# Attention inside a fused diffusion-backbone layer: the score maxima of two heads taken by products on rows 0 to 63 and 64 to 127 of the array, in six pairs of banks per half query tile

## What is computed

```python
def one(qblk):                       # 128 queries at a time
    s = jnp.einsum('bqkgd,bskd->bkgqs', qblk, k).astype(jnp.float32) * scale
    p = jax.nn.softmax(s, axis=-1).astype(v.dtype)
    return jnp.einsum('bkgqs,bskd->bqkgd', p, v)
```

## Time and profile before

| | |
|---|---|
| median of 3 runs | 2532.43 us (2530.58 to 2535.45) |
| the profiled execution | 2528.88 us, its span 2527.0 us |
| TensorE busy | 2432.8 us (96% of the span) |
| VectorE, ScalarE, GpSimd busy | 1187.3, 678.1, 155.7 us |
| mean granted TensorE clock | 0.985 of full speed |
| the attention's groups | 1190.76 to 1441.80 us from the span's start |

### The profile page before, as it was taken

How to read it: one execution, slowest core, us unless ns; L and a number is a source line. 1 busy time by engine, 2 the same in 40 slices (tenths; PEclk the granted TensorE clock), 3 DMA queues, 4 the chain that set the end, 5 groups by cost and what they waited for, 6 DMA issues and landing times. The chain is left out here.

```text
span 2527.0 us, 41706 instructions
## 1 busy us (share of the span) xinstructions
PE 2432.8 (96%) x17387; PEld 2240.3 (89%) x17387; DVE 1187.3 (47%) x1773; ACT 678.1 (27%) x1036; POOL 155.7 (6%) x194
## 2 busy tenths in 40 slices
PE   6999999999999999989999999979999999999998
PEld 4887789999999899888999898869999999999997
DVE  3331111003543667645555476445555555555555
ACT  3321111113332232234444453232112112112112
POOL 0000000001100011112111010110000000000000
PEclk8999999999999999999999999989999999999999
DMA  6224532225453333142002093231011011011012
GB/s 264 107 84 175 196 121 82 97 70 186 165 176 115 134 116 113 56 131 74 17 17 83 19 388 107 99 142 42 33 50 41 33 50 41 33 50 41 33 50 84
DMA packets 98125, 247.19 MB, mean 98 GB/s; under 512 B 12593, under 2 KB 56065, under 8 KB 88657
## 3 DMA queue, kind: packets, MB, share of 16 engines
q1 hardware_dynamic: 61200, 174.69, 20.0%
q10 hardware_dynamic: 32832, 55.46, 5.9%
q0 software_dynamic: 3968, 15.21, 1.6%
HBM read 183.85 MB, written 61.55 MB: 97 GB/s over the span
## 5 line engine op out<-in xcount | busy, mean ns | idle before, releaser
L59 PE MATMUL ps<-zb,wt 128*128 128x384 f32 x2400 | 651.5, 337 | 10.4 <-DVEq L2617 9.1
L59 PEld LDWEIGHTS ps<-zb,wt 128*128 128x128 f32 x2400 | 441.6, 188 | 28.4 <-DVEq L2617 9.5
L2569 DVE TENSOR_TENSOR merged<-merged,ps 128x512 f32<-128x512 f32 x378 | 259.5, 687 | 322.7 <-PE ps L59 320.1
L59 PE MATMUL ps<-xb,wt 128*128 128x384 f32 x1056 | 358.5, 340 | 0.0
L59 PE MATMUL ps<-ys 128*128 128x512 f32 x1056 | 298.2, 394 | 0.0
L59 PE MATMUL ps<-h_hi,fill_whi 128*128 128x384 f32 x672 | 234.7, 349 | 7.0 <-PEq L79 3.6
L59 PE MATMUL ps<-h_hi,fill_wlo 128*128 128x384 f32 x672 | 225.8, 336 | 0.0
L59 PE MATMUL ps<-h_lo,fill_whi 128*128 128x384 f32 x672 | 225.6, 336 | 0.0
L59 PEld LDWEIGHTS ps<-xb,wt 128*128 128x128 f32 x1056 | 198.5, 188 | 17.3
L59 PEld LDWEIGHTS ps<-ys 128*128 128x128 f32 x1056 | 193.3, 188 | 16.6
L59 PE MATMUL ps<-prj_whi,h_hi 128*128 128x512 f32 (+1 forms) x432 | 164.9, 382 | 6.1 <-DVE h_lo L553 6.1
(11 more groups left out here) (348 smaller groups left out, 3708.3 us busy)
## 6 DMA issues: line engine op xcount, KB each, us to landing
wraw<-in_w_ffn_in SPq DMA_DIRECT2D x22, 1024.0 KB, 4.8
prj_raw<-in_w_ada SPq DMA_DIRECT2D x16, 1024.0 KB, 5.9
fill_raw<-in_w_fill SPq DMA_DIRECT2D x30, 512.0 KB, 4.2
bg_dram<-fill_st ACTq DMA_DIRECT2D x72, 192.0 KB, 2.0
xf<-bg_dram POOLq DMA_DIRECT2D x24, 576.0 KB, 7.9
tok_dram<-prj_tst ACTq DMA_DIRECT2D x45, 256.0 KB, 2.1
zf<-in_w_ffn_out SPq DMA_DIRECT2D x22, 512.0 KB, 3.5
prj_raw<-in_w_tok SPq DMA_DIRECT2D x10, 1024.0 KB, 6.5
```

The source lines that it names most:

```text
L59: mm = pe.matmul(out, lhs[a], rhs[b], start=first and n == 0, stop=last and n == 2)
L2569: v.tensor_tensor(dst, dst, ps[:, bank, :], ALU.add).then_inc(added, 1)
```

## The change

`shift_scores` now works on two heads at once. `qpart` is laid out anew, so that after turning the even head of a pair has the high part of its queries on rows 0 to 63, and the odd head on rows 64 to 127. The keys' high part stands on both halves already. A call ("event" below) makes two products of 64 rows and 384 columns, one for each head, into banks 0 and 1, for one third of the keys. There are six events per group instead of four, at steps 1, 2, 3, 5, 6 and 7. The products no longer take in the low part of the queries, so the maxima differ slightly; any value near the maximum serves, since it only shifts the exponent. VectorE reduces the two banks after each event to one maximum per head and third; after events 2 and 5 it reduces the thirds to one, and negates. `split` takes five instructions instead of two.

```diff
-        qpart = [ph.sb(f"qpart{i}", [P, G, H2], F32R) for i in range(KV)]
+        QP = 5 * HD + 2
+        qpart = [ph.sb(f"qpart{i}", [P, G // 2, QP], F32R) for i in range(KV)]
...
-            def shift_scores(n, kv, a):
-
-                if not (isinstance(n, int) and n + a == 0):
-                    pe.wait_ge(sem["mx"], 4 * n + a)
-                for c in SHIFTS:
-                    mm = pe.matmul(ps[:, c, 0:TH], qt[kv][:, a * P:a * P + P], kt[0][:, kv, c * TH:c * TH + TH],
+            def shift_scores(n, kv, e):
+
+                if not (isinstance(n, int) and n + e == 0):
+                    pe.wait_ge(sem["mx"], 6 * n + e)
+                p, c = divmod(e, 3)
+                for b in range(2):
+                    r, at = slice(b * HD, b * HD + HD), slice((2 * p + b) * P, (2 * p + b) * P + P)
+                    mm = pe.matmul(ps[:, SHIFT + b, 0:TH], qt[kv][r, at], kt[0][r, kv, c * TH:c * TH + TH],
                                    start=True, stop=True)
                 mm.then_inc(sem["s1"], 1)
...
-            for a in range(G):
-                shift_scores(0, 0, a)
-                branch(range(20 + a, 21 + a))
+            for e in range(6):
+                shift_scores(0, 0, e)
+                if e % 3 < 2:
+                    u = 20 + e // 3 * 2 + e % 3
+                    branch(range(u, u + 1))
             shifts(0, 0, 1)
...
-                x = qr[:].rearrange("p (a k) d -> p k a d", k=KV)[:, kv]
-                link(v.tensor_copy(qpart[kv][:, :, 1:H1], x))
-                v.tensor_tensor(qpart[kv][:, :, H1:H2], x, qpart[kv][:, :, 1:H1].bitcast(F32), ALU.subtract).then_inc(done, 1)
+                x = qr[:].rearrange("p (a b k) d -> p k a b d", k=KV, b=2)[:, kv]
+                at = lambda i: qpart[kv][:, :, i:i + HD]
+                even, odd = x[:, :, 0], x[:, :, 1]
+                link(v.tensor_copy(at(0), even))
+                link(v.tensor_copy(at(4 * HD + 1), odd))
+                link(v.tensor_copy(at(2 * HD), even))
+                link(v.tensor_tensor(at(HD), even, at(0).bitcast(F32), ALU.subtract))
+                v.tensor_tensor(at(3 * HD + 1), odd, at(4 * HD + 1).bitcast(F32), ALU.subtract).then_inc(done, 1)
...
-            def shift(n, kv, a):
-
-                v.wait_ge(sem["s1"], 4 * n + a + 1)
-                v.tensor_reduce(mx[:, a % 2:a % 2 + 1], ps[:, 0:3, 0:TH], AX.XY, ALU.max).then_inc(sem["mx"], 1)
-                v.wait_ge(sem["mx"], 4 * n + a + 1)
-                v.tensor_scalar(qpart[kv][:, a, 0:1], mx[:, a % 2:a % 2 + 1], -1.0, None, ALU.mult).then_inc(sem["nm"], 1)
+            def shift(n, kv, e):
+
+                p, c = divmod(e, 3)
+                v.wait_ge(sem["s1"], 6 * n + e + 1)
+                v.tensor_reduce(mx3[:, p, :, c], ps[:, SHIFT:SHIFT + 2, 0:TH], AX.X, ALU.max).then_inc(sem["mx"], 1)
+                if c == 2:
+                    v.wait_ge(sem["mx"], 6 * n + e + 1)
+                    link(v.tensor_reduce(mx[:, p], mx3[:, p], AX.X, ALU.max))
+                    v.tensor_scalar(qpart[kv][:, p, 3 * HD:5 * HD + 2:2 * HD + 1], mx[:, p], -1.0, None, ALU.mult).then_inc(sem["nm"], 1)
...
-                        for a in range(G):
-                            shift(2 * i + kv + 1, 1 - kv, a)
-                            if kv and more2 and a == 1:
+                        for e in range(6):
+                            shift(2 * i + kv + 1, 1 - kv, e)
+                            if kv and more2 and e == 2:
                                 norm_a(i + 3)
-                            if kv and more2 and a == 2:
+                            if kv and more2 and e == 3:
                                 norm_b(i + 3, qtab[:, bass.ds(i + 2, 1)].rearrange("p a c d -> p (a c) d"))
```

More of the change, by code:

```diff
@@ L1558, in attention @@
         pt = [ph.sb(f"pt{i}", [P, G * P]) for i in range(3)]
-        mx = ph.sb("mx", [P, 2])
+        mx3, mx = ph.sb("mx3", [P, 2, 2, 3]), ph.sb("mx", [P, 2, 2])
         rs = ph.sb("rs", [P, KV, G])
@@ L1568, in attention @@
         PT, ST, OB = 3, 4, 7
-        SHIFTS = range(0, 3)
+        SHIFT = 0
+        EVENTS = (1, 2, 3, 5, 6, 7)
         use = lambda i, k: 2 + 5 * i + k
@@ L1648, in turn_queries @@
             for a in range(G):
-                mm = pe.transpose(ps[:, bank, a * P:a * P + P], qpart[kv][:, a, 1:H2].bitcast(F32), g.ident[:])
+                at = a % 2 * (3 * HD + 1)
+                mm = pe.transpose(ps[:, bank, a * P:a * P + P], qpart[kv][:, a // 2, at:at + 2 * HD].bitcast(F32), g.ident[:])
             return mm
@@ L1653, in turn_shifts @@
             for a in range(G):
-                mm = pe.transpose(ps[0:H1, bank, a * P:a * P + P], qpart[kv][:, a, 0:H1].bitcast(F32), g.ident[:])
+                at = 2 * HD if a % 2 == 0 else 4 * HD + 1
+                mm = pe.transpose(ps[0:H1, bank, a * P:a * P + P], qpart[kv][:, a // 2, at:at + H1].bitcast(F32), g.ident[:])
             return mm
@@ L1739, in shifts @@
             def shifts(n, kv, u):
-                pe.wait_ge(sem["nm"], 4 * n + 4)
+                pe.wait_ge(sem["nm"], 2 * n + 2)
                 pe.wait_ge(sem["pte"], u)
@@ L1782, in group @@
                     scores(n, kv, j)
-                    if more and j in (1, 3, 5, 7):
-                        a = j // 2
-                        if a == 0:
+                    if more and j in EVENTS:
+                        e = EVENTS.index(j)
+                        if e == 0:
                             pe.wait_ge(sem["pte"], u + 1)
-                        shift_scores(n + 1, nkv, a)
+                        shift_scores(n + 1, nkv, e)
                     if j >= 2:
@@ L2003, in _ @@
             for kv in range(KV):
-                link(v.tensor_copy(qpart[kv][:, :, 0:1], zero[:]))
+                for i in (3 * HD, 5 * HD + 1):
+                    link(v.tensor_copy(qpart[kv][:, :, i:i + 1], zero[:, 0:2]))
             link(v.tensor_tensor(qr[:], qn[:], grow[:, 0, :].unsqueeze(1).broadcast_to([P, AH, HD]), ALU.mult))
@@ L2065, in tile @@
                     if kv == 0 or more:
-                        for a in range(G):
-                            shift(2 * i + kv + 1, 1 - kv, a)
-                            if kv and more2 and a == 1:
+                        for e in range(6):
+                            shift(2 * i + kv + 1, 1 - kv, e)
+                            if kv and more2 and e == 2:
                                 norm_a(i + 3)
-                            if kv and more2 and a == 2:
+                            if kv and more2 and e == 3:
                                 norm_b(i + 3, qtab[:, bass.ds(i + 2, 1)].rearrange("p a c d -> p (a c) d"))
                     normed(2 * i + kv, kv)
-            for a in range(G):
-                shift(0, 0, a)
+            for e in range(6):
+                shift(0, 0, e)
             with v.Fori(0, 6) as i:
-                link.loop(i, 4)
+                link.loop(i, 14)
                 tile(i, True, True)
```

4 lines of the change are left out of this document (2 added, 2 removed).

## The result

| | before | after |
|---|---|---|
| median of the runs | 2533.61 us (2530.58 to 2536.11, 6 runs) | 2770.14 us (2756.98 to 2771.86, 6 runs) |
| the profiled execution | 2528.88 us, span 2527.0 us | 2757.54 us, span 2755.7 us |
| mean granted TensorE clock | 0.985 | 0.905 |

The ratio is 1.0918 (95% interval 1.0903 to 1.0933): the kernel is 9% slower. I had said 2567 us, range 2544 to 2584. The sign was right, the size was not: 237 us more instead of 35.

What follows compares the result with a forecast made beforehand. TensorE, busy throughout each group at full clock, was taken as the bound. 15 groups add 30.2 us and the part ahead of the loop 4.4: 34.6 on 2528.88, 2563.5; the median lies 3.55 higher: 2567 us, range 2544 to 2584.

Steps and rivals of the forecast that it cites:

- An event's 0.58 us, side by side: TensorE, each event: two half-row products overlap, 0.17 us for the pair, 0.58 with shape changes and unhidden weights (0.47 to 0.69).
- serial: Rival: the pair's products run one after the other, 0.17 us more per event, 2579 us; chance 0.13.
- The change of shape: TensorE around each event: 0.10 us into the narrow shape, 0.10 back, 0.10 for the next full weights, unhidden.
- That rival (2545): Rival: the change of shape costs nothing and the pair takes 0.17 us, but waits grow: 2545 us; chance 0.18.
- VectorE's part: VectorE in each group: `split` 1.42 us instead of 0.75, reductions 0.96 us; TensorE waits only at event 1.
- Event 1 waits as forecast: TensorE at each group's second event waits 0.83 us for VectorE's reduction, net 0.72; no waits at later events.
- A group at full clock: Each loop group gets 2.0 us longer (1.29 events, 0.72 wait), 17.6 to 18 us apart; 15 groups, 30.2 us.
- Ahead of the loop: Before the group loop: events 1.1 us, event 3's wait 1.2, `shifts` 1.4, longer `split` 0.67; together 4.4 us.
- The 0.67 us of the longer `split`: Ahead of the loop: the first queries already wait 0.87 us for `split`, so its 0.67 more come on top.
- The step that failed: All loop groups: pieces were priced at the earlier trace's full clock, giving 30.2 us over 15 groups.
- a clock that falls because TensorE idles, which none of my cases has: Sign named for a wrong prediction, in the profile after: TensorE's clock falls through idling; given no size or chance.

Runs made afterwards that it cites:

- a kernel that only adds them: Kernel before with one 128-column product per head for the maxima, plus six unread half-row pairs per group: 2557.06 us, ratio 1.0098.
- one-row product added: Kernel before plus six products of one row and 128 columns of zeros in each group, ahead of the scores: 2560.56 us, ratio 1.0114.
- the full-row twin: Kernel before with one 128-column product per head for maxima, plus six unread all-row pairs per group: 2537.43 us; with 7 us pause ahead of loop 2553.3 us.
- the pause: TensorE waits about 7 us for four GpSimd powers ahead of the loop; added to the kernel before: 2540.8 us, ratio 1.0034.
- the short version: Kernel before with one product of 128 columns per head for the maxima, cached keys only: 2506.13 us, ratio 0.99.
- the version with the short products and a pause of 7 us: Kernel before with one 128-column product per head for maxima, six unread half-row pairs per group and the pause: 2787.64 us, ratio 1.0998.
- the four short products that did not save it: Changed kernel plus one unread product of all 128 rows and 128 columns in steps 1, 3, 5, 7 of each group: 2767.14 us, ratio 1.0904.
- the one-row products: Six per group, kernel before with fewer maxima columns: one of three products, 2546.07 us; one 128-column product, seven runs 2532.49 to 2538.88, three 2678.36 to 2732.6.
- ten runs of one version: Kernel before with one 128-column product per head for the maxima, plus six one-row products per group: seven runs 2532.49 to 2538.88 us, three 2678.36 to 2732.6.

## Why the prediction was right in its pieces and wrong in its size

- **An event's 0.58 us, side by side**: right, 0.58 in the group at full clock, 0.53 on average in a kernel that only adds them. The side by side was open (chance 0.13 for serial): same rows 0.62 us, both halves 0.45. **The change of shape** (0.30): right, 0.29 us taken away with `nil`, 0.24 per one-row product added, its columns left out. That rival (2545) falls.
- **VectorE's part**: right in its times, too high in its cost. `split` 1.40 us (forecast 1.42), the reduction 0.95 (0.96). Event 1 waits as forecast, but adds 0.47 and 0.56 us in the two groups at full clock, not 0.72. In the loop the weight loads of events wait for VectorE 15 times, 10.2 us in all; only in these two groups does the wait hold up the products.
- **A group at full clock**: 17.62 us from one `nil` to the next, where before has 16.01 and 15.62 by turns. That is 1.8 more than their mean, where the sum had 2.0: 1.29 for the events, and the shorter wait. The forecast was 17.6 to 18.
- **Ahead of the loop**: event 3 waits 1.06 us (1.2), `shifts` 1.46 (1.4). The 0.67 us of the longer `split` did not come on top: the first queries wait 0.88, and ScalarE's copy ends it. From the first event to these queries it is 18.37 us against 14.73: 3.6 more, where I had 4.4. Both stretches contain the dip of the clock of 6.8 us.
- **The step that failed** is the one on which the sum rests, that every group runs at the clock of the earlier trace rows. Among what would make the prediction wrong I had put "a clock that falls because TensorE idles, which none of my cases has". It needed a case, with a price: 15 groups at 30.7 us instead of 17.6, and what follows. The earlier trace rows show full clock for a TensorE that never waited; they don't show what happens in groups that wait, with shapes that fill less of the array. And the pauses ahead of the loop, 2.5 us of them new, I had priced as idle time only, though the trace of before has the clock at half for 6.8 us behind a wait of 1.41 just ahead of them.

What the runs put in its place: the long fall takes two things. A *starter*, a wait of TensorE (7 us or 0.9 to 1.5 us ahead of the loop, or 0.4 to 0.9 within the groups, singly or in pairs, and not each time); and groups that *don't bring the clock back*. With groups of full-row products the clock comes back: in the kernel before (8 of 8 runs), the full-row twin (4 of 4), the changed kernel with full rows (4 of 4, with all its waits). With half-row pairs it stays down to the end: 4 of 4 with the pause, and in the profile of the changed kernel, whose six runs all took 2756.98 us or more. Some of its variants come back for 3 to 65 us and fall again. Without a starter the half-row pairs run at full clock, 4 of 4. The pause alone cost 8 us (on the kernel before), the half-row pairs alone 51 (over the short version), both together 282 (2787.64 - 2506.13). That both are needed is shown for the version with the short products and a pause of 7 us. For the changed kernel itself it is argued: from there, from the four short products that did not save it, and from where its falls begin, as no version of it without any wait was run. And the account does not cover the one-row products: with less full work beside them the clock fell in 1 of 6 and 3 of 10 runs, with no wait added; whether one of before's own waits starts it there is not known.

What stays open: which property of the pairs holds the clock down, half of the array's rows at rest or the time lost at the change of shape (an event takes 0.53 to 0.58 us, of which its columns are 0.17). The full-row twin takes away both at once. The one-row products point to the second as at least a part of it, since with less full work beside them they lose the clock in 3 of 10 runs; but one-row products with a pause were not tried. Why two runs of the changed kernel with twelve more products are near 2600 us and two at 2670 and 2682 is open too.

## What to carry to other kernels

Price a change of TensorE's work twice: by the pieces at the clock of the trace, and by what the stretch becomes if the clock halves; and give the second a chance whenever the change both puts waits into a stretch and replaces full products by narrow ones. A wait of half a microsecond can cost far more than half a microsecond then. Read the clock of the trace before around each wait that is there already: here it stood at half for 6.8 us behind one of 1.41. Test such a change with a pause in front: a stretch that recovers in the trace of before may not recover after the change. And look for narrow products in the middle of full ones: a one-row product that costs 0.3 us can be given 128 rows of zeros.

## What the hardware showed that I had not expected

- At half clock TensorE is busy for all of 224 us, with nothing to wait for, and the clock does not rise: 0.50 in every such row. A busy TensorE is no sign of full clock. The Trainium skill, "TensorE: Matmul & The Clock Gate", section "What's actually happening", lets the clock follow how busy TensorE has been; by the busy time that the profile prints, these rows disagree.
- Two waits of 0.43 or 0.44 and 0.69 or 0.70 us, 2.7 us apart, stand in five places of one profile; behind three of them the clock falls. The same page, section "A second HAM failure mode: psum-queue depth-cycling", has short idle times between products that make the clock swing; the trace agrees for these three falls, and adds that it may not swing back.
- The same kernel runs at either clock by chance: ten runs of one version gave seven times 2532 to 2539 us and three times 2678 to 2733.
- Work that nobody needs made a kernel faster: some 33 us of full products added to the changed one took 134 us off its median.
- Two products on opposite row halves overlap wholly (0.45 against 0.62 us), but a pair among full products costs 0.53 to 0.58 us, more than the 0.33 of the two over all rows: half the rows, more time.
